# A hybrid encoder layer on one core: which columns the router's gathering products read, and where five waits stand

## The reference, cut to what matters

```python
h     = rms_norm(x, attn_norm_w)
mem_n = rms_norm(mem, mem_norm_w)                 # 256 memory tokens
proj  = h @ w_in                                   # 2944 columns
y_na  = neighborhood_attention(q, k, v, rpb)       # 8 heads, 8 x 16 window on a 16 x 64 grid
y_rw  = rwkv7_bidirectional(...)                   # 4 heads, forward and backward scan
y_mem = memory_cross_attention(mq, mem_n, ...)     # 4 heads, 256 keys
x     = x + concat([y_na, y_rw, y_mem]) @ w_out
h2    = rms_norm(x, ffn_norm_w)
g     = argmax(h2 @ w_group + b_group)             # one of 4 groups, then the top 2 of its 4 experts
x     = x + sum over 2 experts: weight * (silu(h2 @ w_gate[e]) * (h2 @ w_up[e])) @ w_down[e]
```

## Time and profile before

| what | value |
|---|---|
| median of 3 runs | 1231.07 us (1229.01 to 1234.85) |
| the profiled execution's own time | 1229.47 us |
| its span | 1227.8 us |
| PE busy | 1175.5 us (96%), 10250 matmul records |
| weight loads (PEld) busy | 677.1 us (55%) |
| DVE, ACT, POOL busy | 561.7, 309.9, 213.8 us |
| line 1404, out projection, 256 records of 128x512 | 112.3 us |
| line 1640, collecting, as a share of the chain that ended last | 3% |
| gathers of expert tokens, as a share of that chain | 2% |

### The profile page before, as it was taken

One profiled execution on the slowest core, in us unless ns is written; L12 is line 12 of the kernel. 1 busy time (PEld: TensorE's weight loads), 2 busy tenths in 40 slices (PEclk: granted clock), 3 DMA queues, 4 the chain that ended last, 5 costly groups with the idle time before them and its releaser, 6 DMA issues. The chain is left out here.

```text
span 1227.8 us, 25084 instructions
## 1 busy us (share of the span) xinstructions
PE 1175.5 (96%) x10250; PEld 677.1 (55%) x10250; DVE 561.7 (46%) x1361; ACT 309.9 (25%) x793; POOL 213.8 (17%) x259
## 2 busy tenths in 40 slices
PE   5999999999999888899999999999999999999996
PEld 5534444444444566699995455784444444455553
DVE  4358546899795554555673444634111111111111
ACT  5063114432220666633441221300000000000000
POOL 0201310110000324200000001223254521112220
PEclk9999999999999899999999999999999999999999
DMA  9321522151401733234324741418999998867433
GB/s 330 95 47 47 163 69 67 33 174 44 126 18 51 195 75 110 72 87 116 107 80 172 284 165 70 171 55 359 413 375 348 356 361 343 311 272 283 134 128 110
DMA packets 104988, 209.07 MB, mean 170 GB/s; under 512 B 35636, under 2 KB 70932, under 8 KB 100776
## 3 DMA queue, kind: packets, MB, share of 16 engines
q1 hardware_dynamic: 79832, 129.29, 30.1%
q0 software_dynamic: 17120, 46.69, 11.3%
q10 hardware_dynamic: 7920, 31.46, 7.4%
HBM read 178.24 MB, written 35.58 MB: 174 GB/s over the span
## 5 line engine op out<-in xcount | busy, mean ns | idle before, releaser
L522 PE MATMUL pj_ps<-hT,pj_w 128*128 128x512 f32 x576 | 252.9, 595 | 0.0
L522 PEld LDWEIGHTS pj_ps<-hT,pj_w 128*128 128x128 f32 x576 | 107.8, 190 | 135.4 <-issue 134.9
L1404 PE MATMUL ps_out<-w_out,mixT 128*128 128x512 f32 x256 | 112.3, 594 | 2.1 <-PEq L2620 1.8
L2243 PE MATMUL ex_py<-wd,ex_hT 128*128 128x512 f32 x256 | 113.1, 592 | 0.0
L1404 PEld LDWEIGHTS ps_out<-w_out,mixT 128*128 128x128 f32 x256 | 47.9, 190 | 59.5 <-issue 59.4
L732 DVE RECIPROCAL mixT<-mixT 128x1024 f32<-128x1024 f32 (+1 forms) x11 | 68.9, 6262 | 22.6 <-ACT mixT L652 17.6
L2390 ACT ACTIVATE ex_sg<-ex_pg 128x512 f32<-128x512 f32 x16 | 9.6, 597 | 272.5 <-PE ex_pg L2297 272.5
L2309 PE MATMUL ex_pu<-proj 128*128 128x512 f32 x176 | 78.0, 592 | 0.0
L2297 PE MATMUL ex_pg<-proj 128*128 128x512 f32 x176 | 77.6, 594 | 0.0
L2243 PEld LDWEIGHTS ex_py<-wd,ex_hT 128*128 128x128 f32 x256 | 47.1, 190 | 52.8 <-issue 52.8
L2502 DVE TENSOR_TENSOR ex_hid<-ex_pu,ex_sg 128x512 f32<-128x512 f32 x16 | 11.1, 692 | 141.8 <-PE ex_pu L2309 141.8
(11 more groups left out here) (371 smaller groups left out, 2003.3 us busy)
## 6 DMA issues: line engine op xcount, KB each, us to landing
wd<-in_moe_w_down ACTq DMA_DIRECT2D x15, 2048.0 KB, 9.8
proj<-in_moe_w_gate SPq DMA_DIRECT2D x11, 2048.0 KB, 10.5
proj<-in_moe_w_up SPq DMA_DIRECT2D x11, 2048.0 KB, 12.5
mixT<-in_moe_w_gate SPq DMA_DIRECT2D x5, 2048.0 KB
mixT<-in_moe_w_up SPq DMA_DIRECT2D x5, 2048.0 KB, 10.2
pj_w<-in_w_in SPq DMA_DIRECT2D x18, 512.0 KB, 4.0
proj<-in_x SPq DMA_DIRECT2D x16, 512.0 KB, 10.3
products<-pj_unit POOLq DMA_DIRECT2D x4, 2048.0 KB, 9.9
```

The source lines that it names most:

```text
L522: mm = pe.matmul(ps[:, t % 2, half, :], w_tile(t)[:, n, :], s.hT[:, n, half * 512:(half + 1) * 512], start=(n == 0), stop=(n == KD - 1))
L1404: mm = pe.matmul(s.ps_out[:, t % 2, half * 512:(half + 1) * 512], s.mixT[:, k, t * P:(t + 1) * P], s.w_out[:, k, half * 512:(half + 1) * 5 ...
L2243: mm = pe.matmul(py[:, half, :], hT[:, j, :], wd[e % 2][:, j, half * 512:(half + 1) * 512], start=(j == 0), stop=(j == KF - 1))
```

## The change

1. Projection: POOL sets a one to 1.0 as its first work, and ACT takes its Sqrt before it waits for any rows.
2. Attention: nothing is zeroed first and has a semaphore of its own; pr_near has one too, and only ACT waits for it, at the first neighbourhood step; PE waits for the zeros of ps_t at its first turn, not before its first scores.
3. Router: the collecting matmuls read 128 neighbouring columns of x1, and the gate and up weights of expert 0 alone are loaded in the order "(k p)" (8 pieces of 2 KB on each partition). copy_first takes the norm's weights from the parameters, and the load of s.w_turned is gone. The first 13 instructions of order_experts stand ahead of copy_first.
4. Experts: the tokens of expert 1 are transposed inside the up products of expert 0, ahead of their last two chunks, and DVE copies them before it forms hid(0).
5. End: POOL's waits for all written rows stand behind the loop over further blocks and in its body.

```diff
+        one = sb("one", [P, 1])
+            pool.memset(one[:, :], 1.0).then_inc(one_in, 1)
             pool.wait_ge(row_normed, NORM_TILES)
...
+            act.wait_ge(one_in, 1)
+            act.activation(one[:, :], one[:, :], ACT.Sqrt)
             for n in range(NORM_TILES):
                 act.wait_ge(rows_in[n], 16)
...
+            pool.memset(nothing[:, :], 0.0).then_inc(nothing_in, 1)
             pool.memset(s.ring[:, :, :, :], 0.0).then_inc(s.ring_zeroed, 1)
-            pool.memset(nothing[:, :], 0.0).then_inc(zeroed, 1)
             for R in range(2):
-                pool.memset(pr_near[R][:, :, :], 0.0).then_inc(zeroed, 1)
+                pool.memset(pr_near[R][:, :, :], 0.0).then_inc(near_zeroed, 1)
...
-                if k:
-                    pe.wait_ge(pt_ready, k)
+                pe.wait_ge(pt_ready, k) if k else pe.wait_ge(zeroed, 2)
...
-            pe.wait_ge(zeroed, 5)
...
-            dve.wait_ge(zeroed, 5)
+            dve.wait_ge(nothing_in, 1)
...
+                        if x == len(MEMORY_STEPS):
+                            act.wait_ge(near_zeroed, R + 1)
...
-            sp.dma_start(s.w_turned, s.inp["ffn_norm_w"].rearrange("o (p k) -> p (o k)", p=P)).then_inc(router_in, 16)
...
-            for load in expert_loads(s, STATIC[0], 0, 0):
+            for load in expert_loads(s, STATIC[0], 0, 0, "e (k p) f -> e p k f"):
...
-                    mm = pe.matmul(s.ps_out[:, 0, k * P:(k + 1) * P], interleaved(s.x1[:, t, :], KD)[:, k, :], pick[:, t, :],
+                    mm = pe.matmul(s.ps_out[:, 0, k * P:(k + 1) * P], s.x1[:, t, k * P:(k + 1) * P], pick[:, t, :],
...
-                                  b3(s.w_turned[:, k].unsqueeze(2), [P, KD // 2, P]), ALU.mult).then_inc(s.first_copied, 1)
+                                  b3(s.par("ffn_w", KD)[:, k].unsqueeze(2), [P, KD // 2, P]), ALU.mult).then_inc(s.first_copied, 1)
...
             norm(TT - 1, 1)
+            order_places()
             copy_first(0)
             copy_first(1)
-            order_experts()
+            order_lists()
...
-            for g in range(NG):
-                pool.wait_ge(s.row_written[g], 16 * NE // NG)
-            for u in range(2):
-                pool.wait_ge(s.row_written_o[u], 16 * len(range(u, ROOMS, 2)))
+            def all_written():
+                for g in range(NG):
+                    pool.wait_ge(s.row_written[g], 16 * NE // NG)
+                for u in range(2):
+                    pool.wait_ge(s.row_written_o[u], 16 * len(range(u, ROOMS, 2)))
             def rest(b, i, third, turn):
                 u = (turn + ROOMS) % 2
+                all_written()
...
             overflow(pool, rest, n)
+            all_written()
...
+                    if e == 0 and j == KD - 2:
+                        turn_x(1)
                     mm = pe.matmul(pu[:, :], xT[:, u, j, :], wu[g][:, j, :], start=(j == 0), stop=(j == KD - 1))
                 mm.then_inc(upped, 1)
-                if e < FIRST_ROOM:
+                if 0 < e < FIRST_ROOM:
                     turn_x(e + 1)
...
+                if e == 0:
+                    copy_x(1)
                 dve.wait_ge(silu, e + 1)
...
                 dve.tensor_tensor(hid[:, :], pu[:, :], sg[:, :], ALU.mult).then_inc(hidden, 1)
-                if q < 0:
+                if e and q < 0:
                     copy_x(e + 1)
```

More of the change, by code:

```diff
@@ L235, in projection @@
         spare = sb("spare", [P, 1])
+        one = sb("one", [P, 1])
+        one_in = sem("one_in")
         keep = sb("keep", [P, RWC])
@@ L939, in attention @@
         table_in = [sem(f"table{v}") for v in range(3)]
+        nothing_in, near_zeroed = (sem(n) for n in ("nothing_in", "near_zeroed"))
         zeroed, scored, biased, exped, inverted, scaled, turned, pt_ready, summed, stored = (
@@ L1539, in out_projection_router @@
         spare = s.proj[:, C_ALL - 1, 160:512]
-        s.w_turned, rate, nearest = (spare[:, n * KD:(n + 1) * KD] for n in range(3))
+        rate, nearest = (spare[:, n * TT:(n + 1) * TT] for n in range(2))
         slotf = spare[:, 32:48].rearrange("p (k t) -> p k t", k=2)
@@ L1752, in place, with order_places @@
                 link(dve.tensor_tensor(s.count[:, :], pl[:, 1, 3 * NE:4 * NE], s.count[:, :], ALU.add))
-            def order_experts():
+            def order_places():
                 per = NE // NG
@@ L1771, in order_experts, with order_lists @@
                 link(dve.tensor_tensor(low[:, :], low[:, :], high[:, :], ALU.add))
+            def order_lists():
                 link(dve.tensor_tensor(t256[:, :, :], b3(low[:, :].unsqueeze(1), [P, NE, NE]), b3(iota16.unsqueeze(2), [P, NE, NE]), ALU.is_equal))
@@ L1815, in norm @@
                 if t == 0:
-                    dve.wait_ge(router_in, 96)
+                    dve.wait_ge(router_in, 80)
                 if t >= 2:
@@ L1908, in _, with expert_loads @@
             exponents(PAIRS - 1)
-def expert_loads(s, e, g, u):
+def expert_loads(s, e, g, u, turned="e (p k) f -> e p k f"):
     def load(dst, name, layout, done):
@@ L1916, in load @@
         return lambda eng: eng.dma_start(dst, rows.rearrange("o p k f -> p (o k) f")).then_inc(done, 16)
-    return (load(s.wg[g], "moe_w_gate", "e (p k) f -> e p k f", s.wg_in[g]), load(s.wu[g], "moe_w_up", "e (p k) f -> e p k f", s.wu_in[g]),
+    return (load(s.wg[g], "moe_w_gate", turned, s.wg_in[g]), load(s.wu[g], "moe_w_up", turned, s.wu_in[g]),
             load(s.wd[u], "moe_w_down", "e (k p) f -> e p k f", s.wd_in[u]))
```

## The result

The changed kernel takes **1216.24 us** (median; 1212.3 to 1219.03), the kernel before 1232.12 beside it (1229.01 to 1234.85): ratio 0.987, 95% interval [0.983, 0.991]. A ratio is the time of a kernel by that of the kernel before, run beside it on the same chip. So it is 16 to 17 us faster. The median lies 9.9 us above the forecast of 1206.3, and 2.2 us above the end of its range (1202 to 1214). The profiled execution took 1216.12 us, with a span of 1214.1.

What follows compares the result with a forecast made beforehand. PE, busy 96% of the span, was taken to bound the kernel. Terms of 16.2, 1.3, 1.2, 2.6, 0.8 and 1.9 summed to 24.0 us, giving 1206.3 between 1205.5 and 1207.1, with 8 in 10 expected within 1202 to 1214.

Steps and rivals of the forecast that it cites:

- the attention's 2.6 us: Attention's start: PE's first scores start behind the barrier without the wait for zeros, 2.6 us gained; bounds 1 and 4.5.
- expert 3's gather: Experts: gather issued 19.4 us earlier, PE there 17.5 us earlier, so 1.2 of the 1.38 us wait goes.
- the root's table: Start: both table loads ahead of the first root go; 0.8 us gets through; bounds 0.9 and a loss of 2.5.
- Collecting: Router: records at 0.109 us instead of 0.240, gate of expert 0 starts 16.2 us earlier.
- The price of the moved order: Router: moving order_places costs 0.1 us of PE time, hidden by the collecting; uncovered it would cost 3.2 us.
- rival A: Router: the clock falls in the collecting; 1208.9 us if 40 records are slow, 1217.6 if all; chance 0.14.
- Rival B: Router: collecting stays at 0.240 us, held by something else than the stride; 1223.5 us; chance 0.04.
- Expert 1's transposes: Experts: transposes inside up of expert 0 remove PE's idle ahead of gate of expert 1, 1.3 us gained.
- rival C: Experts: expert 2's weights delay expert 1's gather, a 2 to 10 us stall inside up, 1208 to 1216; chance 0.08.
- rival D: Experts: each gather takes 27.1 us and stands behind the one before, slower than before at 1239.5; chance 0.02.
- The end: End: the loop runs beside the last write's landing, 1.9 us gained; bounds 0 and 2.4.
- a code fetch may lie elsewhere: Attention's start: the reservation, beside a shorter low-clock stretch, behind the bounds 1 and 4.5 on its 2.6 us.

Runs made afterwards that it cites:

- e4: The kernel before with only the router's, the experts' and the end's parts of the change: 1215.48 us, ratio 0.9867.
- e7: The changed kernel with the loads of bias tables 5 to 12 held to later steps of the memory attention: 1199.89 us, ratio 0.9804.
- e6: The kernel before with the attention's part of the change alone: 1221.26 us, ratio 0.9983.
- e16: The kernel before with the loads of bias tables 5 to 12 held to later steps and the attention's part of the change: 1217.37 us, ratio 0.9956.
- warm start: The changed kernel with 34 dummy products on a zeroed tile, 26 ahead of the first transposes and 8 ahead of the keys: 1201.12 us, ratio 0.981.
- e3: The changed kernel without the attention's part, its waits as before: 1215.18 us, ratio 0.9855.
- e2: The kernel before with the root's table part (the early Sqrt) alone: 1236.41 us, ratio 1.0025.
- e15: The kernel before with the loads of bias tables 5 to 12 held to later steps of the memory attention: 1219.84 us, ratio 0.9975.
- e10: The changed kernel with both table loads spread over the memory attention and 34 dummy products at the start: 1210.11 us, ratio 0.9808.
- e11: The changed kernel with spread table loads, 34 dummy products at the start, and dummies in PE's two idle times of the projection: 1206.67 us, ratio 0.9781.

## Why the prediction was wrong

The median is 9.9 us above the forecast. 1.8 us of that are the level (last point below); the other 8.1 are gain that didn't come, 15.9 us for 24.0. **The step that failed first is the attention's 2.6 us**, which the sum passed on to the end and which the stage gave back. Behind it stand the 1.2 us of expert 3's gather and the 0.8 us of the root's table. Of the 8.1 us the two early parts explain their 3.4, by e4's ratio. The rest lies between the collecting and the end: 18.5 us in the profiles' means and 16.4 by that ratio, for 20.6.

**Collecting: right in mechanism, 0.8 us short in size.** 15.4 us came for 16.2 (33.06 less 17.61 is 15.45). A record takes 0.115 and not 0.109 us, and so PE itself, not VectorE's order, holds the gate back by the end. The price of the moved order was hidden, as said. The fall of the clock (rival A) didn't come: 1.00 in every window from 800 us to gate. Rival B's 1223.5 was a us too high by its own terms, for 1206.3 and 16.2 make 1222.5.

**Expert 1's transposes: right**, 1.5 us for 1.3 (from gate to gate 14.6 us for 16.1). Gate of expert 1 starts with no idle; the transposes inside up have no wait for the gather in any of the eleven profiles that have them there, so rival C's stall didn't come either.

**Expert 3's gather: wrong in a step.** I took its issue to come 19.4 us earlier, with the order. But its chain is another one now; in the chain of waits after:

```profile
808.74 1.84 POOL slot_tokens L1609
...
813.43 3.42 DMA slot_tokens<-op_entry,op_slot
...
839.50 0.54 POOL idx L2040
840.04 0.31 issue
840.34 24.82 DMA expert_x<-ffn_rows,idx
865.20 1.09 PE ex_pt L2215 x8
```

The scatters behind place(3) and POOL's index reads, one by one, decide now, not the order. Counted from the first collected record (796.35, and 789.2 before), gather 3 is issued 15.8 us earlier (at 44.0; before at 876.09 - 27.1 - 789.2 = 59.8, by the earlier trace rows), and PE gets there 17.0 us earlier: the room shrank by 1.2 where I had it grow by 1.9. In the seven profiles with collecting and end as before the wait is 0.5 to 1.5 us; in the ten with both changed there is none, or 0.4, in five, 1.6 to 1.8 in three, and 3.5 and 4.2 in two. Behind the two longest the clock falls. Timeline and window of the change's second profile:

```profile
866.32 1.97 PE L2215 MATMUL ex_pt<-cst,expert_x 128*128 128x128 f32 x8 [3.47 <-DMA expert_x<-ffn_rows,idx]
...
865.00:871.00 6.00, 4.68 (x12) 0.51 0.99 416
```

There it is 406.3 us from gate to the end, for 400.1 in the first profile. This is rival D's mechanism in small, at the expert that D named; the mean wait over the ten is 1.3 us where I counted 0.2. The Trainium skill (DMA: Bandwidth & Descriptors, Queues, rings and completion order) says that a DMA engine goes round the queue rows that have work; my estimate from it, that a gather beside the weights keeps about half of the engines, is not borne out. The gather took 24.8 and 27.7 us beside them (up to 30.6 in e7), against 4.4 for the shortest of the earlier trace rows, far more than twice, and the measurement decides.

From the first collected record to the end, the seven take 436.6 to 438.6 us, in the mean 437.4, and the ten 416.1 to 423.9, in the mean 418.9. I forecast 20.6 us for this part; the first pair of profiles gave 20.8, the means give 18.5. The first pair alone hides the miss of 2.1 us.

**The end: right**, 2.8 us for 1.9. The last write goes at 1208.66 and the span ends 5.4 us behind it; it was 8.3.

**The attention's start: the step that failed.** "Without the wait PE starts behind the barrier" is true: the idle time is 2.30 for 5.03 us. I let it through to the end because PE is busy behind it. But 20 us further on the products stood still for 2.03 and 2.41 us, with a clock of 0.50 behind each stall. From the first score to the neighbours' it takes 37.9 to 42.0 us, in the mean 40.1, in the seven profiles with the early attention and the unspread loads (37.9 in e6, where it is the only change, 42.0 with the warm start, 39.5 to 41.2 in the others). In the six where the wait for the zeros stayed it takes 36.0 to 38.4, in the mean 36.8. That is 3.3 us more for the 2.7 that the wait was. The stalls of 0.9 us and more sum up to 4.2 us in the mean of the seven and to 1.5 in that of the six: 2.7 us more, as much as the wait was. In e6 and e16, on the kernel before, the part may keep 2 us; in the changed kernel it keeps none (e3). I had named the cause in a bound ("a code fetch may lie elsewhere") and not priced it, though a stall of 2.05 us stood at 436 us in the trace of before already.

**The root's table: the cover was wrong.** The 1.0 us at the keys came. But PE idled 2.26 us ahead of them, which I had foreseen at 1.5, and the 16 first products took 5.36 us, for 3.62 to 3.72 in the profiles where the clock stayed: the projection began 0.7 us later than before. That is in the bounds (a loss of 2.5), but the sum took the gain. In three of the seven profiles with the early table and no dummies at the start the clock fell there and the projection began 0.3 to 0.7 us later than in the first profile of before (34.19); in the other four it began 0.9 to 1.7 us earlier. The mean of the seven is 0.2 us under that of the eight profiles with the late table (33.75 for 33.96), for 0.8 in the sum.

**The level.** The forecast of 1206.3 is the middle between the profiled execution (1229.47) and the median shown (1231.07), each less 24.0. The kernel before as run beside the change has a median of 1232.12, which would have made 1208.1. So 1.8 us of the miss is no matter of the change at all. The profiled execution was a good one: it had no low stretch in the projection, and only one other of the fifteen profiles shares that. That shows when the first pair of profiles, 13.7 us apart in span, is set against the 24.0. The projection of the changed kernel took 5.0 us more, its start lost 1.5 us against the sum, and its attention 3.5 (2.6 and 0.9 back), which leaves 14.0; the small rest is 0.6 us more in the stages up to the out projection and 0.2 better behind it. The ratios' 16 to 17 are higher, as they would be if most runs of before have the projection's stretches too.

What stays open: why the runs of e2 have the lower clock; what the warm start and the spread loads gain, each alone, on a chip where the plain change is measured too; why the ratios give 16.4 us from the collecting on where the profiles' means give 18.5; and how often the stretches come in either kernel, of which the mean clock of a run tells a sum but not the place.

## What to carry to other kernels

Subtract from the typical run: compare the one profiled time with the median of the runs, look whether its clock was high, and count the low stretches that other executions will have. A stretch that saves microseconds in front of thin work (the attention's small products beside full DMA queues) is not passed on to the end by a busy PE; ask what meets there at the new time, and fill or spread it before you shorten it. The dense term, 128 records by 0.12 us, was safe because the rows for both layouts stood in the trace. And look at PE's short idle times between dense stretches: a few dummy products in two of them were worth 2 to 3 us on one chip (0.9981 beside the kernel before, 0.9781 beside 0.9808). Run each variant beside the one that it is compared with, on one chip; three additions here lack that.

## What the runs showed of the hardware

- A weight load of 128x128 f32 whose columns are 32 bytes apart takes 336 ns, one of neighbouring columns 190 to 192; the strided product takes 0.240 us, at a clock of 0.50 and of 1.00 alike, the other 0.115, seen at 1.00 alone.
- Behind idle times of PE of 1.3 and 2.6 us in the midst of the projection the clock was at 0.50 in 13 of 15 profiles; with dummy products in these idle times in none of three. Some 4.7 us hang on it (363.6 for 368.2), more than the 3.9 of the idle times themselves.
- Stalls of 0.9 to 4.1 us inside a row of small products, released by "issue", end 2.6 to 3.0 us after a 16 KB packet of the instruction queue began, in 20 of 20. With the table loads spread they are gone in two kernels (e7, e15) and stay in three others (1.10 us in e10, 0.91 in e11, 2.07 in e16).
- A gather of 512 KB beside the weight loads took 24.8 us in one profile of the kernel and 27.7 in the other, and whether PE waits for it, and for how long, changes from one execution to the next.
- One stage differs by 8 to 10 us from chip to chip (86 to 88 for 76 to 79 us) while the out projection up to the collecting takes 138.5 us in all profiles but one (140.2).
